# RWKV inverse levels as 64 by 64 tiles, ScalarE's RWKV preparation reordered, key projections moved into the top-k of a hybrid decoder trunk

## What is computed

```python
score = where(key_pos <= q_pos, relu(q_idx . k_idx) summed with weights, MASK)   # B
_, idx = lax.top_k(score, 128); attention over these keys only
# C, per head and token: a recurrence with a rank-one correction
sa = einsum('bhvi,bhi->bhv', S, -kkt)
S = S * wt + sa * (kkt * at) + vt * kt
y = einsum('bhvj,bhj->bhv', S, rt)
```

## Time and profile before

| | |
|---|---|
| median of three runs (lowest to highest) | 2177.32 us (2177.28 to 2185.11) |
| the profiled execution's own time | 2177.14 us |
| its span, first to last instruction | 2175.3 us |
| mean granted TensorE clock | 0.974 of 2.4 GHz |
| busy share PE, DVE, ACT, POOL | 94%, 43%, 35%, 46% |

### The profile page before, as it was taken

One profiled execution on the slowest core, in us unless ns is written; L12 is line 12 of the kernel. 1 busy time (PEld: TensorE's weight loads), 2 busy tenths in 40 slices (PEclk: granted clock), 3 DMA queues, 4 the chain that ended last, 5 costly groups with the idle time before them and its releaser, 6 DMA issues.

```text
span 2175.3 us, 31563 instructions
## 1 busy us (share of the span) xinstructions
PE 2036.3 (94%) x10760; PEld 1601.3 (74%) x10760; DVE 943.5 (43%) x1690; ACT 764.0 (35%) x1178; POOL 1006.7 (46%) x1231
## 2 busy tenths in 40 slices
PE   7999897999999899999899998979999989999995
PEld 5876755878777688888678776567786767888884
DVE  5737856323322513223177478652333315133143
ACT  6334253223542522222363342431244334122224
POOL 4444424212646555557534443422135574455574
PEclk9999998999999999999899999999999999999998
DMA  4122211001222222222212222110011222222222
GB/s 168 69 78 78 78 50 39 30 30 39 69 75 82 78 97 96 96 96 97 79 56 79 87 73 74 48 31 30 30 59 59 78 88 78 97 96 96 96 97 97
DMA packets 50352, 161.72 MB, mean 74 GB/s; under 512 B 5280, under 2 KB 13600, under 8 KB 49952
## 3 DMA queue, kind: packets, MB, share of 16 engines
q1 hardware_dynamic: 49056, 157.05, 21.9%
q10 hardware_dynamic: 1152, 2.86, 0.4%
HBM read 157.79 MB, written 2.10 MB: 73 GB/s over the span
## 4 chain that ended last, share of the span: by engine, by line
issue 54%; POOL 41%; PE 3%; POOLq 1%; DVE 1%; DMA 0%; ACT 0%; SPq 0%; DVEq 0%; ACTq 0%
POOL w_lo L1406 20%; POOL w_lo L1436 16%; POOL slab L1426 2%; PE bank L551 1%; PE bank L553 1%; PE bank L552 1%; POOL rstd L1415 1%; POOL slab L1447 1%; POOLq L1433 0%; POOL slab L1429 0%; DMA w_raw<-wproj 0%; DVE u_lo L1505 0%; POOLq L1402 0%; DVE u_hi L1516 0%; DVE u_lo L1517 0%
## 5 line engine op out<-in xcount | busy, mean ns | idle before, releaser
L1406 POOL TENSOR_TENSOR w_lo<-w_raw,w_hi 128x256 fp32r<-128x256 f32 x624 | 500.6, 833 | 819.4 <-ACT w_hi L1046 819.1
L551 PE MATMUL bank<-hn_hi,w_hi 128*128 128x512 f32 x1312 | 550.8, 420 | 43.6 <-POOL w_lo L1406 21.1
L1436 POOL TENSOR_TENSOR w_lo<-w_raw,w_hi 128x256 fp32r<-128x256 f32 x512 | 379.9, 774 | 303.3 <-ACT w_hi L1366 303.3
L552 PE MATMUL bank<-hn_lo,w_hi 128*128 128x512 f32 x1312 | 518.2, 395 | 0.0
L553 PE MATMUL bank<-hn_hi,w_lo 128*128 128x512 f32 x1312 | 517.8, 395 | 0.0
L551 PEld LDWEIGHTS bank<-hn_hi,w_hi 128*128 128x128 f32 x1312 | 250.4, 191 | 125.3 <-issue 51.9
L551 PE MATMUL bank<-u_hi,w_hi 128*128 128x512 f32 x736 | 298.6, 406 | 24.0 <-POOL w_lo L1398 11.4
L553 PEld LDWEIGHTS bank<-hn_hi,w_lo 128*128 128x128 f32 x1312 | 250.0, 191 | 54.6
L552 PE MATMUL bank<-u_lo,w_hi 128*128 128x512 f32 x736 | 288.6, 392 | 0.0
L553 PE MATMUL bank<-u_hi,w_lo 128*128 128x512 f32 x736 | 288.6, 392 | 0.0
L1366 ACT ACTIVATE w_hi<-w_raw 128x1024 fp32r<-128x1024 f32 x128 | 135.8, 1061 | 429.5 <-DMA w_raw<-wrest 404.2
(11 more groups left out here) (313 smaller groups left out, 2695.6 us busy)
## 6 DMA issues: line engine op xcount, KB each, us to landing
w_raw<-wrest SPq DMA_DIRECT2D x144, 512.0 KB, 3.3
w_raw<-wmerge SPq DMA_DIRECT2D x80, 512.0 KB, 3.5
w_raw<-wproj SPq DMA_DIRECT2D x64, 512.0 KB, 3.5
x<-x_in SPq DMA_DIRECT2D x4, 512.0 KB, 7.1
slab<-rope ACTq DMA_DIRECT2D x2, 1024.0 KB, 4.8
out<-x SPq DMA_DIRECT2D x4, 512.0 KB, 2.6
con<-tables SPq DMA_DIRECT2D x1, 898.0 KB, 11.3
slab<-masks SPq DMA_DIRECT2D x1, 896.0 KB, 12.9
```

The lines of the kernel that those rows point to most:

```text
L551: mm(o_, stat[0], mov[0], start=first, stop=False)
L552: mm(o_, stat[0], mov[1], start=False, stop=False)
L1406: ins = pool.tensor_tensor(wlo[:, s_, cs], wraw[:, s_, cs], whi[:, s_, cs].bitcast(f32), SUB)
L1436: ins = pool.tensor_tensor(wlo[:, s_, cs], wraw[:, s_, cs], whi[:, s_, cs].bitcast(f32), SUB)
```

## The change

- The products of lines 874, 882 and 886 go through `level_product`. At levels 1 to 5 a head's 128 by 128 product becomes two products of 64 by 64 on the diagonal (rows and output partitions 0 to 63, then 64 to 127), each of 32 moving columns; both halves are written to the same PSUM bank. At level 6 it is one product of 64 by 64 with 64 columns. A semaphore increment of PE stands before each group.
- ACT's copy of a level (1308) becomes two copies of 64 partitions by 128 elements; at level 6 it is one copy of 64 partitions. DVE's masked copy at level 6 becomes a plain copy of 64 partitions.
- ACT takes `gate1`'s units 4 and 5 and splits two chunks before the table load for `Ln`, and splits one more chunk between the `Exp` of the key norms and the wide ones.
- `dk` moves from behind `branch1` to before `gate1`; the last round of the top-k gets 16 dense steps (the two units of `dk`). `dk` lies in slab 11 from then on, so the small copy of C goes to slab 10.
- DVE also calls `gated_to` between a round's `max` and its `match_replace`, 3 steps short of the round's own mark.

With `dk` ahead, the places of C start 16 steps later and the limit of 408 is reached at the last chunk's `c_mask` 1: no dense step is left for its 12 level places and 3 `c_out` places.

```diff
-ORDER += [..., ("gate0", 4, 8), ("branch0", 4, 8), ("gate1", 0, 4)]
-ORDER += [("branch1", 0, 4), ("gate1", 4, 8), ("branch1", 4, 8), ("dq", 0, 2), ("dk", 0, 2), ("gate2", 0, 3)]
+ORDER += [..., ("gate0", 4, 8), ("branch0", 4, 8), ("dk", 0, 2), ("gate1", 0, 4)]
+ORDER += [("branch1", 0, 4), ("gate1", 4, 8), ("branch1", 4, 8), ("dq", 0, 2), ("gate2", 0, 3)]
...
-        place(("b_topk", r), FILL["b_topk"][r // 8], ("branch0", KT - 1))
+        place(("b_topk", r), FILL["b_topk"][r // 8] if r + 1 < TOPK // 8 else 16, ("dk", 1))
...
-                    mm(ps[4 + t][:, :], v2w[:, t * P:(t + 1) * P], S(11, 0)[0:32, :], start=True, stop=True)\
+                    mm(ps[4 + t][:, :], v2w[:, t * P:(t + 1) * P], S(10, 0)[0:32, :], start=True, stop=True)\
...
+                        def level_product(bank_, stat, mov, side):
+                            for h in range(H):
+                                if lv == 6:
+                                    lo, to = slice(side * HD, side * HD + HD), slice(HD - side * HD, P - side * HD)
+                                    ins = mm(bank_[to, h * HD:(h + 1) * HD], stat[lo, h * P + HD - side * HD:(h + 1) * P - side * HD],
+                                             mov[lo, h * P + side * HD:h * P + side * HD + HD], start=True, stop=True)
+                                    continue
+                                for r in range(2):
+                                    rs = slice(r * HD, (r + 1) * HD)
+                                    cs_ = slice(h * P + r * HD, h * P + (r + 1) * HD)
+                                    o_ = bank_[rs, h * HD + r * HD // 2:h * HD + (r + 1) * HD // 2]
+                                    ins = mm(packed(o_, n), stat[rs, cs_], halves(mov[rs, cs_], n, side), start=True, stop=True)
+                            return ins
+                        pe.sem_inc(carrier, 1)
+                        level_product(ps[4], LTm, X_, 0).then_inc(*c_pp.up())
                         dense(("c_level", c, lv, 0))
                         pe.wait_ge(*c_ppu.at(L, 6 * c + lv))
+                        pe.sem_inc(carrier, 1)
                         if lv < 6:
+                            level_product(ps[5], XT_, PP, 0).then_inc(*c_xx.up())
+                        level_product(ps[6], PP, XT_, 1).then_inc(*c_xx.up())
                         dense(("c_level", c, lv, 1))
...
-                take(("c_prep", 2))
+                take_steps(REACH[("c_prep", 2)] + 8)
                 act.preload_act_table(ACT.Ln)
                 act.wait_ge(*c_kkv.at(L, 1))
                 link(fn(slab[:, 5, :], slab[:, 5, :], ACT.Ln))
                 fn(slab[:, 5, :], slab[:, 5, :], ACT.Exp, scale=-0.5).then_inc(*c_kkr.up())
+                split_to(INDEX[("gate1", 6)] + 1)
                 act.wait_ge(*c_ex.at(L, 1))
...
-                        fn(halves(tgt, n, side), packed(ps[bk][:, 0:256], n), ACT.Copy).then_inc(*c_xxu.up())
+                        if k_ == 10:
+                            ins = fn(halves(tgt[0:HD, :], n, side), packed(ps[bk][0:HD, 0:256], n), ACT.Copy)
+                        else:
+                            for r in range(2):
+                                rs = slice(r * HD, (r + 1) * HD)
+                                into = tgt[rs, :].rearrange("p (h r b two n) -> p h r b two n", r=2, two=2, h=H, n=n)[:, :, r, :, side, :]
+                                from_ = ps[bk][rs, 0:256].rearrange("p (h r b n) -> p h r b n", r=2, h=H, n=n)[:, :, r, :, :]
+                                ins = fn(into, from_, ACT.Copy)
+                        ins.then_inc(*c_xxu.up())
...
                     link(ins)
+                    gated_to(GATED_TO[("b_topk", r)] - 3)
                     carry_wait()
```

More of the change, by code:

```diff
@@ L48 @@
 ORDER = [(name, 0, n) for name, _, n in PROJ_A + PROJ_B + PROJ_C]
-ORDER += [("gate0", 0, 4), ("branch0", 0, 4), ("gate0", 4, 8), ("branch0", 4, 8), ("gate1", 0, 4)]
-ORDER += [("branch1", 0, 4), ("gate1", 4, 8), ("branch1", 4, 8), ("dq", 0, 2), ("dk", 0, 2), ("gate2", 0, 3)]
+ORDER += [("gate0", 0, 4), ("branch0", 0, 4), ("gate0", 4, 8), ("branch0", 4, 8), ("dk", 0, 2), ("gate1", 0, 4)]
+ORDER += [("branch1", 0, 4), ("gate1", 4, 8), ("branch1", 4, 8), ("dq", 0, 2), ("gate2", 0, 3)]
 ORDER += [("dv", 0, 2), ("gate2", 3, 4), ("branch2", 0, 4), ("gate2", 4, 8), ("branch2", 4, 8), ("gate3", 0, 4)]
@@ L1279, in _ @@
                 act.wait_ge(*c_vh.at(L, 1))
-                fn(S(11, 0)[0:32, :], ps[6][0:32, :], ACT.Copy).then_inc(*c_vhc.up())
+                fn(S(10, 0)[0:32, :], ps[6][0:32, :], ACT.Copy).then_inc(*c_vhc.up())
                 take(("c_prep", 1))
@@ L1871, in _ @@
                         n = LEVELS[lv]
-                        dve.copy_predicated(halves(PPs[lv % 2], n, 0).rearrange("p (h b) n -> p h b n", h=H),
-                                            level_half(1, lv, n, 0), packed(ps[4][:, 0:256], n)
-                                            .rearrange("p (h b) n -> p h b n", h=H)).then_inc(*c_ppu.up())
+                        if lv < 6:
+                            ins = dve.copy_predicated(halves(PPs[lv % 2], n, 0).rearrange("p (h b) n -> p h b n", h=H),
+                                                      level_half(1, lv, n, 0), packed(ps[4][:, 0:256], n)
+                                                      .rearrange("p (h b) n -> p h b n", h=H))
+                        else:
+                            ins = dve.tensor_copy(halves(PPs[lv % 2][HD:P, :], n, 0), packed(ps[4][HD:P, 0:256], n))
+                        ins.then_inc(*c_ppu.up())
                         link(dve.tensor_copy(heads(PPs[(lv + 1) % 2]), over_heads(C("ident"))))
```

## The result

The changed kernel took **2203.86 us**, median of four runs (2202.9 to 2204.96), beside 2177.3 (2176.67 to 2185.11) of the kernel before: ratio 1.0114, 95% interval 1.009 to 1.0137. It is slower, by 1.1%; the forecast was 2154.5, and its range ended at 2176. The profiled execution took 2203.48 us (span 2201.7, mean granted clock 0.945, before 0.974).

What follows compares the result with a forecast made beforehand. PE, busy 94% of the span, was taken as the bound, with its stops and the 1.2 GHz clock behind them. 2177.1 - 31.6 (levels) + 9.0 (dk) + 0 (preparation) + 0 (chunk 3) = 2154.5 us, range 2134 to 2176.

Steps and rivals of the forecast that it cites:

- Levels at full clock: Levels with dense steps, chunks 0 to 2: four-head product 0.44 us, level 3.32 us, 5.3 us less a chunk; -31.6 us.
- rival 3: Level products: tiles do not run side by side, a product stays at 0.88 us; 2196.5 us, chance 0.10.
- rival 4: Filled levels: the clock falls there too; at half the levels some +20 us a layer, above 2190 us; chance 0.05.
- Chunk 3 without dense steps: Last chunk's levels: -7 us a layer at full clock, +7 at 1.2 GHz; clock down for about half, 0.
- rival 2: Chunk 3: the clock is down throughout and into `c_norm`; 2154.5 + 14 = 2168.5 us, chance 0.20.
- Rival 1: Chunk 3: the clock holds, no gap there being over 1 us; 2154.5 - 14 = 2140.5 us, chance 0.22.
- dk into the top-k: 16 steps of `dk` before the attention, 10.9 us a layer, partly filling PE's waits: +5.4 and +3.6, +9.0 us.
- The refund of 2.3 us for the slow clock behind the old stop: Behind the top-k, first layer: filling PE's wait removes 4.6 us at clock 0.50, saving 2.3 us.
- The RWKV preparation: Before the chunks: transposes 3.4 us earlier, 2.6 and 1 us lost at 1.2 GHz; 0, bounds -3.4 and +3 a layer.

Runs made afterwards that it cites:

- e12: The changed kernel with full-array level products in chunk 0 alone: median 2254.8 us (2216.0 to 2263.3).
- e13: e4 with 2 and 3 dense steps in the masks instead of 1 and 1, taken from the preparation's last place: 2147.8 us, ratio 0.9865.
- e17: The changed kernel with 2 and 3 dense steps in the masks instead of 1 and 1, the preparation's last place 8 instead of 20: 2180.8 us.
- e18: e4 with 1 and 3 dense steps in the masks (only the second stop covered), the preparation's last place 12: 2149.4 us, ratio 0.986.
- e6: e4 with one unread full-array matmul of 512 columns more in every level place: 2225.9 us (2203.3 to 2249.7).
- e16: The kernel before with ACT's new preparation order, full arrays, no dense step in the masks, 8 more in the preparation: 2248.2 us, ratio 1.034.
- e4: The kernel before with only the tiles and ACT's new preparation order, dk not moved: median 2182.3 us (2143.0 to 2206.1), ratio 0.993.
- e15: e4 with no dense step in the masks and 8 more in the preparation: 2290.5 us, ratio 1.054.

## Why the prediction was wrong

The forecast was 2177.1 - 22.6; the profiled execution came 26.3 us above 2177.1. From the two tables, over both layers:

- **Levels at full clock, -31.6 predicted.** The mechanism held and its size was a little off. A product is 0.52 us in a pair (0.44 taken), a level 3.46 (3.32), a chunk gives 4.4 us and not 5.3: six chunks -26.4, +5.2 against the sum. *The tiles do not run side by side* (rival 3) is out: a product would have stayed at 0.88 us, and the halves' passes start 7 ns apart. The Trainium skill's TensorEngine Tiling, Gotcha 1 (PSUM Pressure), spoke for that rival; this trace disagrees, for both halves go to one bank here and ran at once.
- **The clock in filled tiled chunks, nothing predicted.** This is the step that failed: "PE is full there, so 0.05" (rival 4). Chunk 0 of both layers ran at 1.2 GHz for 41 us, 17.4 us each over a chunk at full clock: **+34.8**. PE was indeed full while it lasted, so being full did not protect it. A stop of 0.97 us stood right ahead of the first level, which I had not priced because the kernel before has it too (0.9 us) and its profile shows no fall. Full arrays mostly come back from such a fall (after 7 us in e12's chunk 0, after 31 in its second layer), tiles don't until the chunk's end. With that stop covered by dense steps the fall is gone (e13, e17, e18). The rival's price was near (+20 us a layer for half the levels; 17.4 for one filled chunk of three), its chance was not.
- **Chunk 3 without dense steps, 0 predicted.** It took 42.7 us, +4.1 a layer, **+8.2**, with the clock at 0.50 for 34 of them. That is rival 2, at a little over half its price: a bare level at 1.2 GHz takes 4.44 us (4.55 predicted), but the clock was back by the chunk's end, so the 3.7 us behind it (line 935 and the dense work) were not lost. Rival 1 is out: the clock fell in the bare chunk of both layers. The Trainium skill's TensorE: Matmul & The Clock Gate, in Why this matters for your kernels, asks for no long idle gaps, which spoke for rival 1. By that rule the clock would have held in chunk 0 too, where the longest gap between the clock's rise and its fall was 0.97 us; this trace disagrees.
- **dk into the top-k, +9.0 predicted.** First layer +8.3 (line 806 at 327.4 against 319.1) where +5.4 was predicted, second +2.3: **+10.6**. The refund of 2.3 us for the slow clock behind the old stop does not exist: the attention takes 52.8 us without that stretch and 52.5 with it, so PE was not what bound it there. The second layer came out lower ahead of the logits: +7.2 us from the end of the first layer's C to them, for 10.9 us of `dk`. Some 4 us of that are luck, as far as one profile of each kernel tells: in this stretch the kernel before is at 1.2 GHz from 670.6 to 677.4 and from 1076.8 to 1093.8, the changed one has no such stretch at the first place and a shorter one, 1094.7 to 1101.6, at the second. Without them `dk` would have cost some 14.6 us, the term's error would be +5.6, and the sum would be the same.
- **The RWKV preparation, 0 predicted.** The transposes come 3.6 and 2.5 us earlier (3.4 predicted), 1.4 us in each layer is given back at 1.2 GHz (2.6 and 1 predicted): **-3.3**, inside the bounds. ACT's new order worked as forecast to 0.1 us: line 1297 at 352.95, and 344.6 + 8.3 is 352.9; the wait at line 837 is 9.5 ("some 9").

The differences, +5.2 +34.8 +8.2 +1.6 -3.3, make 46.5 of 48.9 us; the other 2.4 lie behind C in the second layer.

Two slips of the prediction's arithmetic change nothing here: 362.94 - 359.4 is 3.5 and not 3.4, and 0.43, 0.22 and a third of 0.20 make a chance of 0.72 and not 0.74.

**What stays open:** why a 64 by 64 product between dense steps keeps the clock down. One tiled product a level is enough, more full-array work beside it doesn't help (e6), and with full arrays the same place recovers. Covering a stop also puts more dense work ahead of the level; e13 and e18 do both at once, and stops of 1.0 to 1.5 us a little earlier in the chunk did no harm there. Why the same stop brings a fall in one chunk and not in the next is open too. And the full-array stretches of 24 to 31 us (e12, e16) say that the difference between the arrays is one of degree.

## What to carry over

Before small tiles take the place of full arrays, look at PE's short stop right ahead of them, in the kernel as it is: here a stop that cost full arrays little put a tiled stretch at half clock until its end. Dense work taken from a place where PE waits anyway covered it, and made the tiles worth 1.35% (e13, 2147.8 us). Repeat a kernel's run ten times before believing a gain that lives on the clock: e4 showed 2143 and 2206 us.

## What the runs showed of the hardware

- PE at 1.2 GHz for 40.5 us in the changed kernel, busy all the time, and for 47.5 us in e15, busy for 46.8 of them.
- Falls came behind stops of 0.97 us right ahead of the first tiled level, in some chunks and not in others of the same execution (e4: one of eight). Stops of 1.53 and 1.50 us earlier in a chunk, with three dense steps behind them, brought none (e18).
- Two row tiles of 64 by 64 wrote halves of one PSUM bank side by side: 32 passes in 1.05 us, two starting 7 ns apart every 58 ns.
- Small products are not all alike at 1.2 GHz: the same bare last chunk took 42.7 us with tiles and 55.0 to 56.2 with full arrays.
